# One transfer per expert: gate, up and down weights of block 1's experts in rows of 24 KB, and another order of their places in SBUF

## What is computed

```python
def _moe(h, w_router_l, bias_l, w_gate_l, w_up_l, w_down_l, w_sh_gate_l, w_sh_up_l, w_sh_down_l):
    scores = jax.nn.sigmoid((xt @ w_router_l).astype(jnp.float32))
    ...
    sel = lax.top_k(cand, TOP_K)[1]
    wts = jnp.take_along_axis(scores, sel, axis=1)
    ...
    def expert_block(args):
        xe, e = args
        return (jax.nn.silu(xe @ w_gate_l[e]) * (xe @ w_up_l[e])) @ w_down_l[e]

    yb = lax.map(expert_block, (xb, block_e)).reshape(n_slots, d)
    routed = jax.ops.segment_sum(yb * slot_w[:, None].astype(yb.dtype), slot_tok, num_segments=t + 1)[:t]
    shared = (jax.nn.silu(xt @ w_sh_gate_l) * (xt @ w_sh_up_l)) @ w_sh_down_l
    return (routed + shared).reshape(b, l, d)
```

## Time and profile before

| | us |
|---|---|
| median of 3 runs | 2906.84 (2905.84 to 2907.74) |
| the profiled execution | 2897.68 |
| its span, first to last instruction | 2896.0 |
| TensorE busy, share of the span | 2550.2 (88%) |
| DMA, mean over the span | 275 GB/s |

### The profile page before, as it was taken

One profiled execution on the slowest core, in us unless ns is written; L12 is line 12 of the kernel. 1 busy time (PEld: TensorE's weight loads), 2 busy tenths in 40 slices (PEclk: granted clock), 3 DMA queues, 4 the chain that ended last, 5 costly groups with the idle time before them and its releaser, 6 DMA issues.

```text
span 2896.0 us, 35205 instructions
## 1 busy us (share of the span) xinstructions
PE 2550.2 (88%) x14664; PEld 1226.6 (42%) x14664; DVE 868.8 (30%) x1539; ACT 434.8 (15%) x940; POOL 462.1 (16%) x374
## 2 busy tenths in 40 slices
PE   6999788899999898889898799959988888888896
PEld 3545556644445444444444345533332223322232
DVE  2045467630235411111111388540211121111212
ACT  2024233210031111111111303410000000000001
POOL 0002444330010343333434101010000000000000
PEclk9999999999999999999999999979999999999999
DMA  5110565342124799999999522359999999999997
GB/s 242 58 58 1 181 223 173 112 167 87 58 91 174 290 379 392 366 346 365 371 392 372 190 109 90 147 196 398 425 425 427 426 426 426 425 427 425 426 427 299
DMA packets 107829, 797.50 MB, mean 275 GB/s; under 512 B 19346, under 2 KB 19778, under 8 KB 56216
## 3 DMA queue, kind: packets, MB, share of 16 engines
q1 hardware_dynamic: 83144, 747.20, 63.2%
q0 software_dynamic: 22688, 39.64, 5.6%
q10 hardware_dynamic: 1840, 8.40, 0.7%
HBM read 769.63 MB, written 39.94 MB: 280 GB/s over the span
## 4 chain that ended last, share of the span: by engine, by line
PE 55%; DMA 30%; DVE 10%; issue 3%; ACT 1%; POOL 1%; SPq 0%; POOLq 0%; ACTq 0%; DVEq 0%
DMA arena<-in_w_down 15%; PE b L3420 8%; DMA yd<-arena 7%; PE b L1641 6%; PE b L2122 5%; PE b L582 4%; PE b L3435 3%; DVE arena L2904 3%; PE b L584 3%; PE b L3460 3%; DMA arena<-in_w_gu 2%; PE b L2140 2%; DMA arena<-h2d,arena 2%; DMA arena<-in_w_mod 2%; PE b L1708 2%
## 5 line engine op out<-in xcount | busy, mean ns | idle before, releaser
L3420 PE MATMUL b<-arena 128*64 128x512 f32 x2048 | 453.1, 600 | 20.2 <-DMA arena<-in_w_up 9.6
L2122 PE MATMUL b<-arena 128*64 128x256 f32 (+1 forms) x3072 | 316.3, 387 | 12.7 <-DMA arena<-in_w_gu 11.3
L3420 PEld LDWEIGHTS b<-arena 128*64 128x64 f32 x2048 | 156.1, 137 | 313.6 <-issue 278.8
L3435 PE MATMUL b<-arena 128*64 128x512 f32 x1024 | 232.2, 597 | 64.1 <-DMA arena<-in_w_down 54.0
L2122 PEld LDWEIGHTS b<-arena 128*64 128x64 f32 (+1 forms) x3072 | 185.7, 131 | 116.8 <-DMA arena<-in_w_gu 13.3
L2481 POOL DMA_INDIRECT yd<-arena x96 | 151.3, 1576 | 317.2 <-ACT arena L2224 145.0
L2140 PE MATMUL b<-arena 128*64 128x512 f32 (+1 forms) x768 | 169.9, 623 | 0.7 <-issue 0.7
L2431 DVE TENSOR_TENSOR arena<-arena,b 128x128 f32<-128x128 f32 x84 | 24.2, 288 | 486.7 <-ACT arena L2217 460.4
L3435 PEld LDWEIGHTS b<-arena 128*64 128x64 f32 x1024 | 72.0, 135 | 223.2 <-issue 115.0
L3558 DVE TENSOR_TENSOR arena<-arena,b 128x512 f32<-128x512 f32 x32 | 20.6, 684 | 470.4 <-PE b L3420 470.4
L1641 PE MATMUL b<-arena 128*128 128x512 f32 x370 | 159.3, 591 | 0.8 <-DVE arena L1451 0.8
(11 more groups left out here) (528 smaller groups left out, 2965.4 us busy)
## 6 DMA issues: line engine op xcount, KB each, us to landing
arena<-in_w_gu SPq DMA_DIRECT2D x65, 2048.0 KB, 8.8
arena<-in_w_down SPq DMA_DIRECT2D x54, 2048.0 KB, 34.1
arena<-in_w_gate SPq DMA_DIRECT2D x48, 2048.0 KB, 38.1
arena<-in_w_up SPq DMA_DIRECT2D x47, 2048.0 KB, 38.8
arena<-in_w_dn SPq DMA_DIRECT2D x65, 1024.0 KB, 10.7
arena<-in_w_mod SPq DMA_DIRECT2D x80, 512.0 KB, 5.3
arena<-in_w_in SPq DMA_DIRECT2D x18, 2048.0 KB, 8.9
arena<-in_w_up SPq DMA_DIRECT2D x34, 1024.0 KB, 36.4
```

What stands on the lines that cost most here:

```text
L2122: x = e.matmul(ps[i % 2][to:to + rows, 0:256], XGT[i % 2][:, k % 4, at:at + rows], GUB[place_of(w)][:, k, j * 256:(j + 1) * 256], start=(k ...
L3420: x = e.matmul(ps[b + c][64 * hf:64 * hf + 64, :], XS[:, kb, (n % 2) * 64:(n % 2) * 64 + 64], w[kb % 2][:, u * 512:u * 512 + 512], start=( ...
L3435: x = e.matmul(p[64 * hf:64 * hf + 64, :], H[:, c * 4 + j, hi * 64:hi * 64 + 64], w[i // 2][:, (i % 2) * 1024 + hf * 512:(i % 2) * 1024 + ...
```

## The change

The two parts of a place become one tile of 24 KB per partition, `places[r]`, with `GUB[r]` and `DNB[r]` as views of it; its address is the same. On the host `w_gu` and `w_dn` become one tensor `w_gd` with rows of 24 KB (and `w_gds` for the shared expert). A load is one transfer of 3 MB with one semaphore, `came_w`; both kinds of matmuls wait for it, and the load waits for the down matmuls of load n-4 (the shared expert's for load 3). Places are taken in the order 2, 0, 1, 2, 3, 0, 1, 2, 3 ...: load 3 takes the place of load 0, and load 4 the one that overlaps the table. The loop for the overflow loads its expert in one transfer too.

```diff
-    GUB, DNB = [], []
-    for _ in range(3):
-        GUB.append(ar(4096).rearrange("p (k n) -> p k n", k=8))
-        DNB.append(ar(2048).rearrange("p (k n) -> p k n", k=2))
+    places = [ar(6144) for _ in range(3)]
...
+    places.append(K.area(ar.at)(6144))
+    GUB = [w[:, 0:4096].rearrange("p (k n) -> p k n", k=8) for w in places]
+    DNB = [w[:, 4096:6144].rearrange("p (k n) -> p k n", k=2) for w in places]
...
     def place_of(w):
-        return (2, 0, 1, 3)[number[w] % 4]
+        return (number[w] - 1) % 4 if number[w] else 2
 
     def freed(e, n, kind):
 
-        if n == 3:
+        if n == 4:
             e.wait_ge(*mm.at("table", 31))
             return
-        w = order[n - 4]
+        w = order[max(n - 4, 0)]
...
         if n >= 3:
-            freed(e, n, "gu")
-        e.dma_start(GUB[r], I["w_gu"][bass.ds(ex, 1)][0] if w else I["w_gus"]).then_inc(*came_gu[r].up(w))
-        if n >= 3:
             freed(e, n, "dn")
-        e.dma_start(DNB[r], I["w_dn"][bass.ds(ex, 1)][0] if w else I["w_dns"]).then_inc(*came_dn[r].up(w))
+        e.dma_start(places[r], I["w_gd"][bass.ds(ex, 1)][0] if w else I["w_gds"]).then_inc(*came_w[r].up(w))
...
-        e.wait_ge(*came_gu[2].at(0))
+        e.wait_ge(*came_w[2].at(0))
...
-                    e.wait_ge(*came_gu[place_of(w)].at(w))
+                    e.wait_ge(*came_w[place_of(w)].at(w))
...
-                    e.wait_ge(*came_dn[place_of(w)].at(w))
+                    e.wait_ge(*came_w[place_of(w)].at(w))
...
     def ov_sp(e, k):
-        freed(e, k, "gu")
         freed(e, k, "dn")
...
-            e.dma_start(GUB[place_of(None)], I["w_gu"][bass.ds(ex, 1)][0]).then_inc(o["w"], 16)
-            e.dma_start(DNB[place_of(None)], I["w_dn"][bass.ds(ex, 1)][0]).then_inc(o["w"], 16)
+            e.dma_start(places[place_of(None)], I["w_gd"][bass.ds(ex, 1)][0]).then_inc(o["w"], 16)
```

More of the change, by code:

```diff
@@ L1946, in experts @@
     WK = K.tiny(32)
-    fourth = K.area(ar.at)
-    GUB.append(fourth(4096).rearrange("p (k n) -> p k n", k=8))
-    DNB.append(fourth(2048).rearrange("p (k n) -> p k n", k=2))
+    places.append(K.area(ar.at)(6144))
+    GUB = [w[:, 0:4096].rearrange("p (k n) -> p k n", k=8) for w in places]
+    DNB = [w[:, 4096:6144].rearrange("p (k n) -> p k n", k=2) for w in places]
     PP = ar(4096).rearrange("p (n u j) -> p n u j", n=32, u=2)
@@ L1980, in experts @@
     came_wr, came_rb = S.dma("wrt"), S.dma("rbias")
-    came_gu, came_dn = [S.dma(n) for n in ("gu0", "gu1", "gu2", "modw4")], [S.dma(n) for n in ("dn0", "dn1", "dn2", "modw5")]
+    came_w = [S.dma(n) for n in ("gu0", "gu1", "gu2", "modw4")]
     came_xg, yout = [S.dma(f"xg{i}") for i in range(6)], [S.dma(f"yout{i}") for i in range(4)]
@@ L2165, in shared_y @@
         if n == 0:
-            e.wait_ge(*came_dn[2].at(0))
+            e.wait_ge(*came_w[2].at(0))
         else:
@@ L2566, in ov_pe @@
             e.wait_ge(o["xc"], i + 1)
-            e.wait_ge(o["w"], i * 32 + 32)
+            e.wait_ge(o["w"], i * 16 + 16)
             for k in range(8):
@@ L3681, in gu @@
         return np.stack([g, u], 4).reshape(-1, 8, 128, 512).transpose(0, 2, 1, 3)
-    A["w_gus"] = gu(f("w_sh_gate"), f("w_sh_up"))[0]
-    A["w_gu"] = gu(f("w_gate")[0], f("w_up")[0])
     dn = lambda m: m.reshape(-1, 2, 128, 1024).transpose(0, 2, 1, 3)
-    A["w_dns"] = dn(f("w_sh_down"))[0]
-    A["w_dn"] = dn(f("w_down")[0])
+    both = lambda a, b: np.concatenate([a.reshape(-1, 128, 4096), b.reshape(-1, 128, 2048)], 2)
+    A["w_gds"] = both(gu(f("w_sh_gate"), f("w_sh_up")), dn(f("w_sh_down")))[0]
+    A["w_gd"] = both(gu(f("w_gate")[0], f("w_up")[0]), dn(f("w_down")[0]))
     A["ctx_2"] = f("ctx_2")[0]
```

## The result

| | us |
|---|---|
| before, median of 5 runs beside it | 2905.84 (2902.78 to 2907.74) |
| after, median of 5 runs | 2949.29 (2940.88 to 2954.85) |
| ratio | 1.0162, 95% interval 1.0145 to 1.0178 |
| profiled execution after: its time, its span | 2954.85, 2953.1 |

The change makes the kernel 1.62% slower, 47 us of 2905.84 (the medians lie 43 us apart). Forecast were 2919.3 and a range up to 2940: the sign was right, the size far too small.

What follows compares the result with a forecast made beforehand. Transfers, not arithmetic, were taken to bound the routed experts' stage. The terms 19.5 - 3 - 4 gave +12.5 us, 2910.2 for the profiled execution and 2919.3 with 9.2 us to the median; range 2897 to 2940.

Steps and rivals of the forecast that it cites:

- Part 1: Order of places: loads 3 and 4 still leave together after the slot-table stores, so the new order costs 0.
- Part 2: Routed experts: one 3 MB transfer released after the down matmuls makes b blocks start later, +19.5 us, less 3 for stores.
- credit of -3: Gaps in the weight queue after releases: stores run unshared there, -3 us, bounds 0 and -8.
- three releases: Releases at 1244.99, 1416.22 and the last one, priced at 6.5 us each; the other eight at 0.
- Part 3's credit: Weight transfers: fewer, longer packets in 24 KB rows save 0.012 us each, taken as -4 us.
- Rival (d): Weight transfers: 24 KB rows travel in pieces, so Part 3 is 0; sum +16.5, 2923 us; chance 0.07.
- rival (c): Stores beside weights: queue 0 gets half the turns and starves; +16 to +37, 2923 to 2944 us; chance 0.13.
- Its sign in the waits: ScalarE's waits for stores: more than the 190.8 us before would show rival (c).

Runs made afterwards that it cites:

- e1_places: The kernel before with only the new order of places for the loads, two transfers and two releases kept: 2905.74 us, ratio 1.0000.
- e5_late_whole: The kernel before, two transfers kept, with gate-up loads released only after the down matmuls and gate-up matmuls waiting for down weights too: 2922.76 us, ratio 1.0057.
- e2_late: The kernel before, two transfers kept, with the gate-up transfer too waiting for the last down matmuls of its place: 2907.06 us, ratio 1.0020.
- e12_whole: The kernel before, two transfers and two releases kept, with gate-up matmuls waiting for the down weights too: 2910.42 us, ratio 1.0039.
- e3_one_8k: The kernel after, still one transfer per expert, with each row in three pieces of 8 KB: 2931.25 us, ratio 1.0101 to the kernel before.
- e6_one_12k: The kernel after, still one transfer per expert, with each row in two pieces of 12 KB: 2918.12 us, ratio 1.0040 to the kernel before.
- e9_after_staggered: The kernel after with a four-expert item's blocks ordered a, a and b, b, s, t: 2947.08 us, ratio 1.0160 to the kernel before.
- e8_before_staggered: The kernel before with a four-expert item's blocks ordered a, a and b, b, s, t: 2905.74 us, ratio 0.9998.
- e10_after_empty_stores: The kernel after with most accumulating stores made empty by rows out of bounds: 2900.50 us, ratio 0.9995 to the kernel before.

## Why the prediction was wrong

**Part 1 held.** After, loads 3 and 4 leave together, behind the two slot-table stores, as predicted:

```profile
980.79 0.36 SPq L2042 DMA_DIRECT2D slotd<-arena  x1
981.20 0.43 SPq L2043 DMA_DIRECT2D slotd<-arena  x1
982.38 1.48 SPq L2021 DMA_DIRECT2D arena<-in_w_gd  x2
```

e1_places measured it at 1.0000.

**Part 2 held in its sum, in part by luck.** It gave +19.5 and a credit of -3; e5_late_whole measured 16.5 us (its interval is 12 to 21). At the last release, 1615.97 us in the chain, TensorE's rows are (start us, us; idle before and releaser in brackets):

```profile
1627.86 5.55 PE L2116 MATMUL b<-arena 128*64 128x256 f32 x32 [5.51 <-DMA arena<-in_w_gd]
...
1636.06 3.68 PE L2116 MATMUL b<-arena 128*64 128x256 f32 x32
```

The a block waited 5.51 us (forecast some 4), the b block started 20.1 us after the release (forecast 17 to 22), 6.7 us more than 13.42 (forecast 6.5). The places are not fully those of the forecast: three releases were priced, and TensorE now waits for weights 12 times. So the sum agrees better than its terms: in e2_late and e5_late_whole too weights are late more often than at three releases (20 and 22 times), while gathers and stores hold up less: in e5_late_whole 54 us more for weights, 43.8 less for gathers and 10.3 more of busy time. The credit of -3 was far too small and so was the +19.5, and the two errors nearly cancel. The prediction read TensorE's 11.3 us for weights and not its 50.8 for gathers, the wait that this change moves.

**The first failed step: Part 3's credit.** It took -4 us for fewer packets, from 0.012 us a packet between two stretches. Half the packets gone, the engines worked 475.1 us on the weights instead of 474.8 (in e12_whole and e5_late_whole, with the packets of before, it is 477 to 478, so the reading is good to some 3 us). The stages with 8 KB rows bear the price out at the short end: e3_one_8k, 0.733 x 658.01 = 482.3 us for 25069 packets, against 475.9 for e6_one_12k's 17041, 0.013 us each. The slope ended above that, and Part 3 went on with it beyond the rows it was read from. Rival (d) named the right worth, 0, for the wrong reason: rows do travel whole (from 980 to 1600 us queue 1 has 8596 packets, for 181.74 MB; forecast some 9,500).

**The second, and the one that decided: rival (c) set against Part 2, not beside it.** The prediction had the mechanism, half the turns for queue 0, and wrote that "part 2 falls away" since weights have then landed anyway, and gave it 0.13. The runs show both: 16.5 us for the waits (e5_late_whole) and some 30 for the rows (the rest to 1.62%; 35 by e6_one_12k), 27.8 us of them as TensorE's idle time for gathers. At 16.5 + 30 the forecast would have been 2953. The weight of it stood in the rows already: queue 1's 18085 packets beside queue 0's 20187 are close to one for one, and the change halves the first. That the engines deal out packets one for one was not known then, as the prediction says; but the count was there to be made on that condition, and instead (c) was priced as a tenth to a fifth of the store pieces of the chain.

**Its sign in the waits was wrong too.** (c) was to show as more of ScalarE's 190.8 us; it fell to 57.7. TensorE's own waits for weights stand ahead of ScalarE's, and the starved transfers show where they come last: as gathers, as GpSimd's wait for a store, as single pieces of 25 to 36 us in the chain. Nor does ScalarE's wait measure the starving: with weights out of the way it is 172.3 us in e9_after_staggered, and 272.5 in e8_before_staggered, which loses nothing.

**A term was missing: the clock.** The windows over the wait at the last release and over the block behind it:

```profile
1620.60:1627.80 7.20, 1.75 (x9) 0.42 (x5) 0.53 (x1) 0.85 (x2) 2.54 (x2) 0.80 1.00 381
1627.80:1633.50 5.70, 5.64 (x33) 3.18 (x34) 0.00 (x0) 0.04 (x1) 1.57 (x1) 0.66 1.03 434
```

0.66 of 2.4 GHz lies between the levels of 1.2 and 2.4, so part of the stretch ran at either, and the 32 matmuls of the a block take 5.55 us there instead of 3.68 at full clock. Over the stage TensorE is 18.6 us longer busy, at 0.92. Which of it is on the path, beside the transfers, and whether it is a cause or only follows the holes, no run here separates: e6_one_12k had 7.0 us of it left for 0.40%, e5_late_whole 10.3 us for 0.57%.

The range ended at 2940 because (c) had been kept apart from Part 2; Part 2's sum and (c)'s upper end together, 16.5 + 37, would have reached 2960.

## What to carry to other kernels

Where two queues share full engines, count each one's packets in the stretch, not only its bytes: the engines here gave them turns one for one, so lengthening one queue's rows takes turns from the other. The row lengths that lost least were those at which both queues had about equally many packets (18061 and 17041 beside 20600). At 9026 the queue of small rows starved; at 25069 and 26071 no gather was late in the stage and the kernels were slower all the same, for a reason only partly found in the waits for weights. Compare kernels by all the waits of the engine that counts, here TensorE's for weights and for gathers, and not by a neighbour's. And a rival that acts in other stretches than the forecast's main term belongs in the sum beside it, not in its place.

## What the runs showed of the hardware

A row of 24 KB is one packet of queue 1: the stage's 196.96 MB are at most 8014 such rows, and it has 9026 packets, the rest small. Each keeps its engine for about 0.95 us (475.1 us x 16 / 8014, an estimate). Where both queues had work all the time, their packets were one for one at rows of 24 KB (245 to 244), of 12 KB (1164 to 1157 in e6_one_12k, 1050 to 1091 us) and of 16 and 8 KB mixed (1874 to 1865). These three layouts cost the engines the same within 3 us, 475 to 478 for 197 MB; with all rows of 8 KB it was 481 to 482. Rows of an indirect store that lie beyond its bound still take a packet each (20604 packets in e10_after_empty_stores, 20603 with all rows stored).
